# A room of 64 bytes at the right end of the on-chip memory moves the weights' split parts

## What is computed

```
proj = rmsnorm(x) @ w_in                        # 1024 -> 6 * 512 + 1100 + 3 * 1024 columns, twice
x = x + y @ w_out;  x = x + square(relu(rmsnorm(x) @ w_up)) @ w_down          # twice, 4096 wide
x = layer_norm(ALPHA * x + gated_deltanet(x));  x = layer_norm(ALPHA * x + swiglu(x))   # 2816 wide
x = layer_norm(ALPHA * x + swa_sink_attention(x))
x = layer_norm(ALPHA * x + moe_swiglu(x))       # 8 experts, 3584 wide
```

## Time and profile before

| | us |
|---|---|
| median of 3 runs (lowest, highest) | 2525.15 (2522.0, 2527.97) |
| the profiled execution | 2525.5 |
| its span | 2523.8 |
| TensorE busy, share of the span | 2405.0, 95% |
| VectorE busy | 1754.7, 70% |
| ScalarE busy | 1418.8, 56% |
| mean granted TensorE clock | 0.979 |

### The profile page before, as it was taken

The page is one execution under the profiler, slowest core; times in us unless marked ns, Lnnn a source line. Parts: engine busy times, 40 slices in busy tenths (PEclk is TensorE's granted clock), DMA queues, the critical chain, the costliest instruction groups (busy, mean ns, idle before and its releaser), DMA issues. The chain is left out here.

```text
span 2523.8 us, 34493 instructions
## 1 busy us (share of the span) xinstructions
PE 2405.0 (95%) x13735; PEld 2047.4 (81%) x13735; DVE 1754.7 (70%) x2029; ACT 1418.8 (56%) x1625; POOL 136.7 (5%) x176
## 2 busy tenths in 40 slices
PE   6999999999998999998998989999999999999996
PEld 6697789888777998787998867888888888888885
DVE  3357655544676555576545568898899889888987
ACT  3544544453454445434434556777777777777775
POOL 0102200000121000060000000000000000000000
PEclk9999999999999999899999989999999999999998
DMA  8243455533344555405556249999999999999996
GB/s 283 104 144 132 156 188 185 190 134 120 132 153 178 183 185 143 94 1 194 174 187 206 85 133 322 367 367 363 358 365 365 358 355 366 365 357 358 366 364 218
DMA packets 391568, 586.59 MB, mean 232 GB/s; under 512 B 21168, under 2 KB 284656, under 8 KB 391280
## 3 DMA queue, kind: packets, MB, share of 16 engines
q1 hardware_dynamic: 391408, 584.38, 68.3%
HBM read 580.14 MB, written 4.19 MB: 232 GB/s over the span
## 5 line engine op out<-in xcount | busy, mean ns | idle before, releaser
L3402 DVE TENSOR_TENSOR moe_low<-ring,moe_high 128x2048 fp32r<-128x2048 f32 x288 | 658.8, 2290 | 98.6 <-ACT moe_high L3363 94.4
L3363 ACT CAST moe_high<-ring 128x2048 fp32r<-128x2048 f32 x288 | 548.4, 1907 | 156.0 <-PE bank L3287 81.1
L3287 PE MATMUL bank<-moe_high,moe_xh 128*128 128x512 f32 x896 | 240.6, 390 | 7.9 <-PEq L3112 7.9
L3287 PE MATMUL bank<-moe_high,moe_xl 128*128 128x512 f32 x896 | 240.3, 390 | 0.0
L3287 PE MATMUL bank<-moe_low,moe_xh 128*128 128x512 f32 x896 | 240.0, 390 | 0.0
L3287 PEld LDWEIGHTS bank<-moe_high,moe_xh 128*128 128x128 f32 x896 | 168.5, 188 | 43.1 <-issue 8.1
L3287 PEld LDWEIGHTS bank<-moe_high,moe_xl 128*128 128x128 f32 x896 | 168.8, 188 | 35.2
L3287 PEld LDWEIGHTS bank<-moe_low,moe_xh 128*128 128x128 f32 x896 | 168.5, 188 | 35.0
L2069 DVE TENSOR_TENSOR chain_low<-ring,chain_high 128x2048 fp32r<-128x2048 f32 x48 | 110.0, 2292 | 116.7 <-ACT chain_high L2042 116.7
L2042 ACT CAST chain_high<-ring 128x2048 fp32r<-128x2048 f32 x44 | 84.1, 1912 | 141.0 <-PE bank L2013 107.1
L3293 PE MATMUL bank<-moe_high,moe_hh 128*128 128x512 f32 x448 | 129.0, 410 | 2.3 <-DVE moe_hl L3407 2.3
(11 more groups left out here) (519 smaller groups left out, 4855.7 us busy)
## 6 DMA issues: line engine op xcount, KB each, us to landing
ring<-in_moe_w_gate SPq DMA_DIRECT2D x199, 512.0 KB, 5.5
ring<-in_moe_w_up SPq DMA_DIRECT2D x199, 512.0 KB, 7.0
ring<-in_moe_w_down SPq DMA_DIRECT2D x95, 1024.0 KB, 7.6
ring<-in_w_in SPq DMA_DIRECT2D x22, 2048.0 KB, 8.1
ring<-in_w_down SPq DMA_DIRECT2D x14, 2048.0 KB, 7.8
ring<-in_w_up SPq DMA_DIRECT2D x10, 2048.0 KB, 8.1
xT<-in_moe_w_down SPq DMA_DIRECT2D x18, 1024.0 KB, 7.5
xT<-in_moe_w_gate SPq DMA_DIRECT2D x31, 512.0 KB, 5.5
```

The lines of the kernel that those rows point to most:

```text
L3287: mm = pe.matmul(core.banks[i % 2][:], (xl if other_low else xh)[:, place(m), 4 * part + c, :], wt[:, c, :], start=(part == 0 and j == 0 a ...
L3363: act.copy(unit(high, u), ring.raw(u)).then_inc(s["weight_high"], 1)
L3402: dve.tensor_tensor(unit(low, u), ring.raw(u), unit(high, u), ALU.subtract)\
```

## The change

One buffer of 16 float32 per partition (64 bytes), which nothing reads or writes, is taken at the right end before any other, for the whole program. So the four buffers that are taken from that end start 64 bytes lower: `high[0]` at 221088, `low[0]` at 212896, `high[1]` at 204704, `low[1]` at 196512; modulo 128 that is 32 and modulo 2048 it is 1952, as for `x_high`. The buffers of the left side stay where they are, and no instruction, wait or DMA is added, removed or reordered.

```diff
@@ -70,6 +70,7 @@
 UNITS = 4
+RIGHT_ROOM = 16
 LAG = 2
@@ -125,6 +126,7 @@
         self.norm_small = self.sbuf("norm_small", [P, 15 * NT + 1])
+        ctx.enter_context(nc.sbuf_tensor("right_room", [P, RIGHT_ROOM], F32, side="right"))
```

## The result

The changed kernel takes 2548.86 us (median of 4 runs, 2542.58 to 2552.69) against 2525.75 of the kernel before (4 runs, 2522.0 to 2527.97): a ratio of 1.010, 95% interval 1.0084 to 1.0116, so 23.1 us slower. The profiled execution took 2552.69, with a span of 2550.7. The forecast was 2518.0 (2516 to 2542); the rival "equal offsets hold 256 columns at 120 ns" had 2546.6.

What follows compares the result with a forecast made beforehand. TensorE, busy for 95% of the span, was taken as the bound, so only the pace of matmuls could count. The terms -3.3 - 1.1 - 0.9 - 2.2 = -7.5 us took 2525.5 to 2518.0, range 2516 to 2542.

Steps and rivals of the forecast that it cites:

- equal offsets hold 256 columns at 120 ns: Rival: all L2013, L907 and L917 matmuls slow to 120 ns; +21.1 us, 2546.6 us; chance 0.20.
- term 4: 4752 matmuls with 256 moving columns (L2013, L907, L917): 2.2 us less, between 4.5 less and 30.9 less 4.5 more.
- Term 1: 1416 matmuls with 512 columns (L2023, L776) reach the expert pace, 226.7 instead of 229.0 ns: 3.3 us less.
- term 2: L1079, 288 matmuls in short runs: up to some 4 ns each, 1.1 us less, bounds 0 and 1.1.
- Term 3: L1842, the branch outputs, 288 matmuls, operand starts still unequal: 0.9 us less, half of a possible 1.9.
- Term 5: The splits (cast and subtraction) writing the moved buffers, DMA, and the experts' matmuls at unmoved addresses: nothing.
- The slow side: Rival: equal offsets hold 256-column matmuls at 120 ns, 6.5 ns each; everywhere +21.1 us, 2546.6 us; chance 0.20.
- Only behind waits: Rival: only projections (L907, L917), starting after a wait, turn slow; +5.9 us, 2531.4; chance 0.23, shared with other mixtures.
- Nothing happens: Rival: stages differ by instruction order, not addresses; all terms 0, time 2525.5 us (2523 to 2528); chance 0.22.

Runs made afterwards that it cites:

- after: The changed kernel: an unused 64-byte buffer at the right end, against the kernel before; 2548.86 us against 2525.75, ratio 1.010.
- room32: Unused room of 32 bytes at the right end instead of 64, against the kernel before; 2548.51 us, ratio 1.008.
- room96: Unused room of 96 bytes at the right end instead of 64, against the kernel before; 2544.14 us, ratio 1.008.
- room224: Unused room of 224 bytes at the right end instead of 64, against the kernel before; 2547.16 us, ratio 1.0091.

## Why the prediction was wrong

**The step that failed is term 4**, the 4752 matmuls of 256 columns. It was taken as -2.2 us and measured +26.0. The bound on its far side was 30.9 - 4.5 = +26.4, which is what came: the pace of the gathering, everywhere. The bound was read rightly from the one row that had the pair of addresses of the change; the choice between the bounds was wrong, and it was made by an argument instead of by the nearest row. Two reasons were given. That the earlier trace rows is a short run entered from half clock: it was no accident of its start, since every block of after has its pace, whether behind a wait (33.51) or behind a stream of 512 columns (367.07). Nor was it the only such place in the old trace: L3070 comes 16 more times in the expert stage, at full clock and straight behind other matmuls, with distances of 116 to 121 ns and 118.3 on average. But with eight matmuls each they are too short to decide, as L2013's blocks in the gated MLP also begin with some distances of 117 to 123 before they reach 113.3. The earlier trace rows was the one row to go by. The second reason was that the beginning decides: this holds at d = 64, between 113.3 and 117.8, as the repeated executions show; at d = 0 there was no second pace to fall into.

**Term 1** was right in its direction: L2023 went from a mean distance of 229.1 to 227.5 ns, -1.7 us. Of L776 and L1079 (term 2 as well) came 229.9 to 228.6, -0.8. Together -2.5 against -4.4. The 2.3 ns per matmul came in the middle of a run (226.9 ns), but the means of the whole trace hold the first matmuls of each run, which are disturbed as in the earlier trace rows, and the sum had counted these too.

**Term 3**, L1842, was taken as -0.9 and came as +0.2 (233.2 to 234.1). The pair went from d = 224 to d = 160, both slow places of the table. That it could lose was said; why half of the gain was taken, no row had given a reason.

**Term 5** was right: the cast 1904 ns and the subtraction 2291 (1912 and 2292 before), and the experts at unmoved addresses kept the pace of the earlier trace rows, 243 us for the same two of them.

**The rivals.** The slow side was right in its place, its price (+21.1 forecast, +23.1 between the medians) and its condition, the equal offsets, and had a chance of 0.20. "Only behind waits" was wrong: the up projections behind the down projections are as slow as the rest. "Nothing happens" fell with the runs too. Moving only `x_high` (x64) or only the weights' parts (after) gives the same 120.0 ns, so the relation of the two addresses is worth 1% of this kernel. The Trainium skill (SBUF — State Buffer, Who interferes with whom) gives TensorE two independent read ports and says that it never waits on anyone. The measured paces, 113.3 against 120.0 ns at 256 columns and 226.7 against 234 at 512 with nothing changed but a start address, don't fit two reads that have no bearing on each other; where in the chip they meet, no run shows. One sum of the slow side was wrong: the gains to be eaten are 5.3 + 4.5 = 9.8 us, not some 12, so it would have decided from 9.8 / 6.5, some 1500 matmuls, and not from 1800. With all 4752 slow, that made no difference.

**The range** ended at 2542, inside the band of the slow side (+12 to +22, so 2537.5 to 2547.5), and the measured 2548.86 lies above the whole band. Cutting off its upper part followed from the chances, but the chance of 0.20 was too low: the only row at the address pair of the change should have outweighed two arguments about it.

## What to carry to other kernels

When a change puts two operands in a new relation, look for the place in the old trace where that relation already exists, with the same instruction size, and let its row decide the term; an argument that the row is special needs a row of its own. Before and after of any edit that adds or resizes a buffer, compare the distance between starts of long matmul runs, for a shift of all buffers behind it can cost more than the edit gives. What is best for one size (equal starts for 512 columns) can be worst for another (256), so count the matmuls of each size before moving a buffer that both use.

## What the runs showed of the hardware

For the float32r matmuls of this kernel, with weights and activations both in the on-chip memory, the pace depends on the start of the moving operand minus that of the stationary one, modulo 256 bytes (seen in steps of 32 bytes; that the sign counts is seen with 256 columns). It lies between 113.3 and 120.0 ns with 256 moving columns and between 226.7 and 234 ns with 512. 128 bytes are not a period, and weights' parts that start at a multiple of 64 bytes (room32), of 128 (room96) or of 256 (room224) brought nothing by themselves: 118.3, 116.7 and 117.3 or 118.7 ns.

At one and the same difference, 64, there are two steady paces with 256 columns, 113.3 and 117.8 ns. Most blocks keep one of them to their end, behind a short pause within a block it can be the other, and which it is changes between executions of the same kernel. So a reading from one execution, as the earlier trace rows were, tells the paces that exist but not how often each is met.

Still open: what in the chip makes the pace depend on the difference, why 0 is best for 512 columns and among the worst for 256, and what decides between 113.3 and 117.8. That the pace of the stream ahead takes part in it is supported by nine executions (63 of 63 short blocks begin at 117.8 behind 227 ns, 110 of 126 at 113.3 behind 229 or 233), but no run changed that pace alone: the room before `mlp_hh` moved its neighbours too.
